# Last attention of a two-block transformer: sink additions, gate splits and two weight splits to GpSimd, first output panel brought forward among the units

## What is computed

```python
def sink_softmax(scores, sink):
    m = sink
    for s in scores:
        m = jnp.maximum(m, jnp.max(s, axis=-1))
    exps = [jnp.exp(s - m[..., None]) for s in scores]
    den = jnp.exp(sink - m)
    for e in exps:
        den = den + jnp.sum(e, axis=-1)
    return tuple(e / den[..., None] for e in exps)
...
    o = o.reshape(bsz, t_lat, AT_Q).astype(h_lat.dtype)
    y_lat = (o * jax.nn.silu(zl)) @ w_out
```

## Time and profile before

| what | us |
|---|---|
| median of 3 runs (1966.79 to 1968.38) | 1968.23 |
| the profiled execution's own time | 1967.3 |
| its span, first to last instruction | 1965.1 |
| units in full flow, 1888.2 to 1930.2 | 42.0 |
| output panels, 1939.1 to 1961.5 | 22.4 |

### The profile page before, as it was taken

The page is one execution under the profiler, slowest core; times in us unless marked ns, Lnnn a source line. Parts: engine busy times, 40 slices in busy tenths (PEclk is TensorE's granted clock), DMA queues, the critical chain, the costliest instruction groups (busy, mean ns, idle before and its releaser), DMA issues. The chain is left out here.

```text
span 1965.1 us, 31270 instructions
## 1 busy us (share of the span) xinstructions
PE 1927.1 (98%) x12652; PEld 1618.6 (82%) x12652; DVE 1303.8 (66%) x2407; ACT 904.7 (46%) x1635; POOL 52.4 (3%) x78
## 2 busy tenths in 40 slices
PE   7999999999999999999999999999999999999998
PEld 5788668889888888898689899998887788888867
DVE  5547777857886665667766777675566464555886
ACT  4446863325423232355764655443443432234685
POOL 0000000001000000000000000000000000001000
PEclk9999999999999999999999999999999999999999
DMA  8322016543545455443139455554311133432411
GB/s 314 117 85 100 18 52 233 179 160 108 193 175 207 177 193 191 166 150 108 54 136 336 172 191 196 177 186 161 119 54 54 65 118 119 150 128 86 150 45 44
DMA packets 53583, 278.39 MB, mean 142 GB/s; under 512 B 4536, under 2 KB 19128, under 8 KB 24512
## 3 DMA queue, kind: packets, MB, share of 16 engines
q1 hardware_dynamic: 47168, 265.50, 37.5%
q10 hardware_dynamic: 6128, 10.03, 1.7%
q0 software_dynamic: 144, 0.85, 0.1%
HBM read 274.26 MB, written 2.11 MB: 141 GB/s over the span
## 5 line engine op out<-in xcount | busy, mean ns | idle before, releaser
L640 PE MATMUL ps<-t 128*128 128x512 f32 (+1 forms) x1936 | 665.2, 344 | 2.4 <-DVE t L2035 2.4
L642 PE MATMUL ps<-t 128*128 128x512 f32 (+1 forms) x1936 | 659.0, 340 | 0.0
L641 PE MATMUL ps<-t 128*128 128x512 f32 (+1 forms) x1936 | 659.0, 340 | 0.0
L2035 DVE TENSOR_TENSOR t<-t 128x1024 fp32r<-128x1024 f32 (+2 forms) x370 | 413.9, 1159 | 153.1 <-ACT t L1386 152.2
L1386 ACT ACTIVATE t<-t 128x1024 fp32r<-128x1024 f32 (+3 forms) x376 | 358.3, 1001 | 194.3 <-PE ps L642 142.6
L640 PEld LDWEIGHTS ps<-t 128*128 128x128 f32 x1936 | 363.6, 188 | 52.5 <-issue 5.1
L642 PEld LDWEIGHTS ps<-t 128*128 128x128 f32 x1936 | 363.6, 188 | 42.5
L641 PEld LDWEIGHTS ps<-t 128*128 128x128 f32 x1936 | 363.7, 188 | 41.8 <-issue 0.7
L2021 DVE TENSOR_TENSOR t<-t 128x256 f32<-128x256 f32 (+9 forms) x622 | 227.9, 386 | 134.3 <-ACT t L1770 31.2
L2030 DVE SCALAR_TENSOR_TENSOR t<-t 128x256 f32<-128x256 f32 (+4 forms) x372 | 272.8, 765 | 34.1 <-ACT t L1491 21.9
L1491 ACT ACTIVATE t<-ps 128x512 f32<-128x512 f32 (+2 forms) x239 | 112.9, 494 | 289.2 <-PE ps L642 187.3
(11 more groups left out here) (191 smaller groups left out, 2278.4 us busy)
## 6 DMA issues: line engine op xcount, KB each, us to landing
t<-in_panels SPq DMA_DIRECT2D x231, 1024.0 KB, 4.9
t<-in_panels SPq DMA_DIRECT2D x12, 768.0 KB, 4.4
t<-in_panels SPq DMA_DIRECT2D x16, 512.0 KB, 3.6
t<-in_window ACTq DMA_DIRECT2D x4, 768.0 KB, 4.5
t<-gates_between ACTq DMA_DIRECT2D x4, 512.0 KB, 4.8
t<-in_panels SPq DMA_DIRECT2D x1, 1088.0 KB, 5.0
t<-in_ctxT SPq DMA_DIRECT2D x1, 1024.0 KB, 6.7
t<-in_xT SPq DMA_DIRECT2D x1, 1024.0 KB, 8.9
```

The lines of the kernel that those rows point to most:

```text
L640: e.matmul(o, hi[:, k, w], xh[:, c0:c1], start=k == 0, stop=False)
L641: e.matmul(o, hi[:, k, w], xl[:, c0:c1], start=False, stop=False)
L642: t = e.matmul(o, lo[:, k, w], xh[:, c0:c1], start=False, stop=k == p.nk - 1)
L2035: e.tensor_tensor(p.half(p.split(wlo), a), p.half(raw[p.slot], a), p.half(p.split(whi), a).bitcast(F32), ALU.subtract).then_inc(*up(ve, (" ...
```

## The change

- `atz` 3 and `atw` 0 go into `POOL_PANELS`: their `lo` is made on POOL. A new POOL function `sink_units` also takes the sink's addition, the denominator's addition, and the whole of `gate_hi` and `gate_lo` (a copy and a subtraction) for the first seven blocks.
- The gate of panel 3 is written as z / (1 + exp(-z)): ACT takes the exponential (no other table), POOL adds 1, DVE takes the reciprocal and multiplies. ACT loads the exponential's table between the query blocks. On DVE the gate moves from i = 1 to i = 2.
- On DVE the second unit's scaling comes ahead of the third unit's maximum.
- The query blocks go into banks 4 to 7; only four of them come ahead of the units, the other four after the scores of unit 0. Gate(3) goes into banks 6 and 7.
- ACT makes the hi of `atw` 0 ahead of the units. PE does the products of `atw` 0 for blocks 0 to 5 within steps 16 to 18, then block 6, two blocks of `atw` 1, block 7, and the rest.

```diff
-POOL_PANELS = [("uq", 0, 0), ("uq", 1, 0), ("atkv", 0)]
+POOL_PANELS = [("uq", 0, 0), ("uq", 1, 0), ("atkv", 0), ("atz", 3), ("atw", 0)]
...
+                query_features(0)
+                def among(i):
+                    if i == 0:
+                        query_features(4)
+                    if i == 1:
+                        gate(3, (6, 7))
+                    if i >= 16:
+                        out_products(0, ((0, 1, 2), (3, 4), (5,))[i - 16])
...
+                softmax("A", at_units(), aPT, among)
+                out_products(0, (6,))
+                out_products(1, (0, 1))
+                out_products(0, (7,))
+                out_products(1, range(2, 8))
...
-                        e.activation(sz[:, c, :], banks(("atz", c))[:, 0:256], ACT.Sigmoid).then_inc(*up(se, ("asig", c)))
+                        f, m = (ACT.Sigmoid, 1.0) if a < 3 else (ACT.Exp, -1.0)
+                        e.activation(sz[:, c, :], banks(("atz", c))[:, 0:256], f, scale=m).then_inc(*up(se, ("asig", c)))
...
                 for c in range(8):
+                    if c == 4:
+                        own()
+                        e.activation(root[:, :], epst[:, :], ACT.Exp).then_inc(*up(se))
...
+                hi_to(at["atw", 0].i)
                 softmax("A", at_units(), aPT, ast, among_units)
...
                 for i in range(n_u + 4):
+                    early = s == "A" and i == 2
+                    if early:
+                        scale(i)
                     if i < n_u:
+                        maximum(i)
+                    if 1 <= i <= n_u and not early:
+                        scale(i)
...
-                        e.wait_ge(*done(("asig", c)))
+                        e.wait_ge(*done(("asig" if a < 3 else "one more", c)))
+                        if a == 3:
+                            e.reciprocal(sz[:, c, :], sz[:, c, :]).then_inc(*up(ve))
+                            own()
                         tt(sz[:, c, :], banks(("atz", c))[:, 0:256], sz[:, c, :], ALU.mult, ("read", ("atz", c)))
...
+            def sink_units():
+                units = at_units()
+                spot = spots(units)
+                lo(at["atw", 0], (0,))
+                for i in range(len(units) + 3):
+                    if i == 2:
+                        for c in (6, 7):
+                            e.wait_ge(*done(("asig", c)))
+                            e.tensor_scalar(sz[:, c, :], sz[:, c, :], 1.0, None, ALU.add).then_inc(*up(po, ("one more", c)))
+                    if 1 <= i <= len(units):
+                        r, es = ast[1][:, spot[i - 1]], ast[2][:, spot[i - 1]]
+                        e.wait_ge(*done(("exp", "A", i - 1)))
+                        e.tensor_tensor(r, r, es, ALU.add).then_inc(*up(po, ("den", "A", i - 1)))
+                    if i == 2:
+                        lo(at["atw", 0], (1,))
+                    if i < len(units):
+                        m, es = ast[0][:, spot[i]], ast[2][:, spot[i]]
+                        e.wait_ge(*done(("max", "A", i)))
+                        e.tensor_tensor(es, m, units[i]["sink"], ALU.add).then_inc(*up(po, ("sink", "A", i)))
+                    if i % 2 == 0 and 4 <= i < 18:
+                        c = i // 2 - 2
+                        e.wait_ge(*done(("az", c)))
+                        e.tensor_copy(aYh[:, c, :], sz[:, c, :]).then_inc(*up(po))
+                        e.wait_ge(po.sem, po.n)
+                        e.tensor_tensor(aYl[:, c, :], sz[:, c, :], aYh[:, c, :].bitcast(F32), ALU.subtract).then_inc(
+                            *up(po, ("aylo", c)))
...
             norm_mod("s1", "cl")
+            lo(at["atz", 3])
+            sink_units()
```

More of the change, by code:

```diff
@@ L1358, in attention_layer @@
                                 t.then_inc(*up(pe, ("full", ("atw", 2 * a + j))))
-                    used(p)
+                    if 7 in ks:
+                        used(p)
+                softmax("A", at_units(), aPT, among)
[3 more added lines that the diff above has]
+                out_products(1, range(2, 8))
+                banks.next(4)
+                for a in range(2, 4):
+                    out_products(a, range(8))
             e.wait_ge(*done("ones"))
@@ L1961, in among_units @@
                         gate(3)
-                    if i in (16, 17):
-                        hi_to(at["atw", i - 16].i)
+                    if i == 17:
+                        hi_to(at["atw", 1].i)
+                hi_to(at["atw", 0].i)
                 softmax("A", at_units(), aPT, ast, among_units)
@@ L2201, in softmax, with maximum @@
                 n_u, spot = len(units), spots(units)
+                def maximum(i):
+                    u, par = units[i], i % 2
+                    both = psum[:, 2 * par:2 * par + 2, :]
+                    e.wait_ge(*done(("full", ("s", s, i))))
+                    m = nm[:, spot[i]]
+                    mv = m.rearrange("p (g x) -> p g x", g=2)
+                    if u["bias"]:
+                        e.wait_ge(*u["bready"])
+                        near = st[2][:, spot[i]]
+                        for g in range(2):
+                            v = banks(("s", s, i, g))[:, 256:512]
+                            e.tensor_tensor_reduce(v, v, u["bias"][g], 1.0, NEG, ALU.add, ALU.max, near[:, g:g + 1]).then_inc(*up(ve))
+                        e.tensor_reduce(mv, both[:, :, 0:256].rearrange("p g (x n) -> p g x n", x=1), AX.X, ALU.max,
+                                        negate=True).then_inc(*up(ve))
+                        own()
+                        stt(m, near, -1.0, m, ALU.mult, ALU.min, ("max", s, i))
+                    else:
+                        e.tensor_reduce(mv, both.rearrange("p g (x n) -> p g x n", x=u["xs"]), AX.X, ALU.max, negate=True).then_inc(
+                            *up(ve, ("max", s, i)))
+                    if u["rms"] is not None:
+                        own()
+                        tt(mv, mv, u["rms"], ALU.mult, ("max", s, i))
+                    if u["sink"] is not None:
+                        own()
+                        tt(m, m, u["nsink"], ALU.min, ("max", s, i))
@@ new lines, in scale @@
+                def scale(i):
+                    u, par = units[i - 1], (i - 1) % 2
+                    r = rs[:, spot[i - 1]]
+                    e.wait_ge(*done(("den" if u["sink"] is not None else "exp", s, i - 1)))
+                    e.reciprocal(r, r).then_inc(*up(ve))
+                    own()
+                    w = 512 // u["xs"]
+                    for g in range(2):
+                        for x in range(u["xs"]):
+                            v = work[:, 2 * par + g, x * w:x * w + w]
+                            c = g * u["xs"] + x
+                            ts(v, v, r[:, c:c + 1], None, ALU.mult, None, ("p", s, i - 1))
@@ L2708, in among_units @@
                 def among_units(i):
-                    if i == 1:
+                    if i == 2:
                         gate(3)
-                    if i in (16, 17):
-                        lo_to(at["atw", i - 16].i)
+                    if i == 17:
+                        lo_to(at["atw", 1].i)
                 softmax("A", at_units(), ast, among_units)
@@ L2764, in gpsimd, with lo @@
         def gpsimd(e):
-            def lo(p):
-                for a in range(2):
+            def lo(p, halves=(0, 1)):
+                for a in halves:
                     e.wait_ge(*done(("hi", p.i, a)))
```

33 lines of the change are left out of this document (17 added, 16 removed).

## The result

| | median us | profiled execution us | its span us |
|---|---|---|---|
| before, beside it on the same chip | 1967.76 | 1967.3 (the one of the earlier trace rows) | 1965.1 |
| with the change | 1973.24 | 1974.73 | 1972.9 |

Slower: the ratio is 1.0028, 95% interval 1.0020 to 1.0037, so +5.5 us (+3.9 to +7.3). 1974.5 was predicted. The profiled execution of the changed kernel lies 1.5 us above its own median, so the terms that follow, all read from it, add up to more than the medians' difference.

The account below looks back on a forecast made before the run. DVE was taken to set the pace of 3.23 us a unit. Start +10.3, pace -1.5 and end -2.3 gave +6.5 us, rounded to about +6.3: median 1974.5 us, 8 in 10 between 1966.5 and 1981.

Parts of the forecast that it names:

- Step 1: Start: POOL's lo of `atz` 3 stalls DVE's second rotation; queries rotated at 1880.4 instead of 1876.4, +4.0 us.
- Step 2: Start: query blocks wait for gate(2)'s reads of their banks; scores of unit 0 at 1882.0 instead of 1878.61, +3.4 us.
- Step 3: Start, ACT: copies, table load and hi of `atw` 0 put the first exponential at 1886.9, not 1881.72, +5.2 us.
- Step 4: Start: late denominator and POOL's half panel delay unit 1's scaling; maximum of unit 2 at 1896.0 instead of 1888.21, +7.8 us.
- the disputed price: Unit 1's scaling on DVE: multiplications by a column wait for POOL's half panel, taken at 2.2 us, bounds 0 and 2.4.
- Step 5: Start: gate(3)'s reciprocals and products, 4.3 us on DVE, put unit 3's maximum at 1901.8; +10.3 us in all by unit 2's transposes.
- The pace: Units 2 to 13: DVE relieved, PE's 3.02 us the floor, 3.09 instead of 3.23 a unit; -1.5 us over eleven.
- The end: Last units: products fill 3.1 us of PE's waits, a new wait of about 0.8 for block 7; -2.3 us.
- hardly meet: Rival at the start: POOL's half panels don't stop DVE; -0.8 us, 1967.4, chance 0.20 with halfway cases up to +3.
- POOL becomes the bound: Rival in the units: small POOL instructions over 0.3 us make its chain the limit; +9 to +14 us, chance 0.15.
- Faster: the start is free: Rival at the start: no conflict, gate's reciprocals fall into a DVE wait; -3.8 to -6 us, 1962 to 1964.4, chance 0.08.

Follow-up runs that it names:

- e1: Changed kernel with the lo of `atz` 3 back on DVE: 1969.93 us, ratio 1.0011 against the kernel before.
- e4: Kernel before the change, with POOL also making the lo of `atz` 3 ahead of DVE, which waits and makes it again: 1973.73 us, ratio 1.0033.
- e2: Changed kernel with POOL's second half of `atw` 0's lo placed after the sink of unit 2: 1972.05 us, ratio 1.0025 against the kernel before.
- e8: e5 with the output panels' products all behind the units: 1963.96 us, ratio 0.9980 against the kernel before.
- e5: Changed kernel with `atz` 3's lo on DVE, `atw` 0's second half lo after unit 2's sink, gate 3 by sigmoid: 1962.01 us, ratio 0.9974 against before.
- e7: Changed kernel with 39 unused matmuls filling PE's long wait ahead of the query transposes: 1972.33 us, ratio 1.0025 against the kernel before.
- e9: e5 with sink and denominator additions and gate splits back on DVE and ACT: 1969.90 us, ratio 1.0012 against the kernel before.
- e10: e9 with DVE making the rest of gated block 6 ahead of the rest of `atw` 1: 1966.46 us, ratio 0.9996 against before.

## Why the prediction held, step by step

The sign, the place and the mechanism were right, and 1973.24 lies 1.3 us from 1974.5; 0.5 of that is the median before, 1967.76 beside it instead of 1968.23, so +5.5 stands against +6.3. But one term was missing, and part of the agreement is luck: errors that cancel. The changed kernel's trace runs ahead of the old one by about 0.6 us before this part (POOL's lo starts at 1872.29, where I had put it at 1872.9).

| step | predicted | in the profile |
|---|---|---|
| 1: queries rotated | 1880.4 | 1879.24 |
| 2: scores of unit 0 | 1882.0 | 1881.53 |
| 3: first exponential | 1886.9 | 1887.86 |
| 4: maximum of unit 2 | 1896.0 | 1897.04 |
| 5: maximum of unit 3 | 1901.8 | 1902.80 |
| transposes of unit 2 | 1904.7 | 1905.54 |
| pace, eleven units | -1.5 | -1.4 |
| end | -2.3 | -2.0 |

- **Step 1** was a little high: the rotations lost 3.5 us, not 4.0. Its own terms give that: 1878.1 and five of 0.36 make 1879.9, +3.5, not 1880.4. I laid only the second rotation beside POOL; the first was already caught, 2.2 of the 3.5. e1 and e4 show the price both ways.
- **Step 2** held: PE's wait of 5.30 ends with gate(2)'s first read, whose banks the query blocks now use.
- **Step 3** was 1.0 short, 1.6 with the earlier trace. Here the missing term enters: at half the clock the scores and the second four blocks take about twice as long, and ACT's copies, hi and exponential stand behind them.
- **Step 4**, the disputed price, was right at its upper end: the pair loses 1.9 us (2.74 against 0.88), and e2 shows that POOL is the cause. The additions of 1 take 0.87, not 0.6, and gate(3)'s matmuls, themselves at full clock, end about 1 us late (1892.6 instead of 1891.5) behind the scores and blocks at half of it; together that puts the denominator at 1893.95 instead of 1892.8.
- **Step 5** held to a tenth: 1902.80 - 1897.04 = 5.76 between the two maxima, against 1901.8 - 1896.0 = 5.8.
- **The pace** came out right for a wrong reason. The floor was not 3.02: the ten units after the third take 2.944 each, and so 2.9 us less than before. The first, at half the clock, takes 1910.28 - 1905.54 = 4.74, 1.5 more than before. The 3.02 that I read between two starts without a printed wait still held about 0.08 of waiting. And POOL's chain, which I had even with DVE's 1.6 us, takes 0.40 + 0.73 + 0.20 = 1.3.
- **The end**, too, is near for a partly wrong reason. The wait for block 7 is 0.32, not 0.8. I had the products fill 3.1 us of waits, but e8 puts only 0.7 of the gain on them: without them its end takes 33.95 us where the kernel before takes 35.16, so 1.2 come with the rest of the change (the wait before the transposes of unit 14 is 1.12 there instead of 1.70).
- **The term left out** is TensorE's clock. I had a wait of PE lengthening by 4 us in step 1 and did not ask what PE does after it; the trace before shows none of it: its waits in this part go to 1.70, and its clock stays at 1.00.

Of the rivals, *hardly meet* falls by the rows of 2.74, 3.51 and 4.72. (Its -0.8 did not follow from its terms either: 4.5 less 1.5 and 2.3 is +0.7.) *POOL becomes the bound* falls by its own condition, small instructions over 0.3 us. POOL by form, 1886 to 1965 (count, busy us, mean ns, idle), beside the earlier trace rows:

```profile
L2841 POOL TENSOR_TENSOR t<-t 128x256 fp32r<-128x256 f32 x7 | 5.1, 729 | 0.6
...
L2829 POOL TENSOR_TENSOR t<-t 128x2 f32<-128x2 f32 x16 | 3.2, 197 | 12.8 <-ACT t L1543 12.8
...
L2839 POOL CAST t<-t 128x256 fp32r<-128x256 f32 x7 | 2.8, 398 | 8.8 <-DVE t L2047 8.8
L2825 POOL TENSOR_SCALAR t<-t 128x256 f32<-128x256 f32 x2 | 1.7, 871 | 1.9 <-ACT t L1966 1.9
```

They take 0.20. *Faster: the start is free* is not what this change does, but it is what e5 is: with the start mended, 1962.01, at the lower end of the 1962 to 1964.4 that this rival gave.

Open is what the low clock costs in the median. Its stretches are no peculiarity of the profile: the mean granted clock is 0.996 in each of the nine executions that the ratio counts, and 0.997 in seven of e7's eight. Within one kernel, executions with less clock are longer: e9's spans are 1965.4 us at a mean of 1.000, 1966.3 to 1966.9 at 0.999 and 1967.6 to 1969.4 at 0.998, e5's 1959.3 to 1960.2, 1961.6 to 1961.7 and 1962.7. That goes with a price for the clock but does not prove one, since a longer wait both lengthens an execution and lowers the clock. The clock's low level and its cause are shown, and so is that the matmuls behind it take longer; its price in the median is not.

## What to carry to other kernels

Small instructions are worth moving from a busy DVE to GpSimd: here the additions of 128x2, at 0.20 us each, and the gate splits of 128x256 gave 3.2 us over eleven units. A long two-input one (2.4 us) did no harm beside a DVE reciprocal or a DVE read of PSUM, and did beside a tensor-tensor and a tensor-scalar; it belongs behind the small ones that others wait for. When an edit lengthens a wait of TensorE, look at the granted clock after the wait and at the durations of the next matmuls, not at the wait alone. Before a difference of 2 us is put down to an edit, see whether it stands where the edit is: most of e8's did not. And price the cheap form of a function on the engine that must finish it: two reciprocals and two additions, with the waits and the lower clock that they brought, cost 5.9 us more here than the table loads that they saved.

## What the runs showed of the hardware that I had not expected

- TensorE's granted clock fell to 0.50 (1.2 GHz) after a single wait of 5.30 us, and again after waits of 1.60 and 2.85 us with 0.71 us of transposes between them (0.52 over 1900.80 to 1910); 1.4 us after the 2.35 us of e9 it fell to 0.50 too. Filling the first wait kept it at 1.00. Shorter waits went either way: at one and the same place it fell after 1.82 us in e1 and 1.79 in e8 (0.73 and 0.69 in 1879 to 1884) and stayed at 1.00 after 1.81 in e5 and 1.80 in e10. What decides there, no run shows.
- On POOL a one-input addition of a constant to 128x256 takes 0.87 us, longer than a two-input subtraction of that size (0.73) and than a rounding copy (0.40).
- Even two-input DVE instructions of 128x2 wait for the end of a POOL instruction. In e5, what is left of the conflict (DVE's row, then POOL's):

```profile
1882.67 2.05 DVE L2047 TENSOR_TENSOR t<-t 128x2 f32<-128x2 f32 x2
...
1882.11 2.40 POOL L2796 TENSOR_TENSOR t<-t 128x1024 fp32r<-128x1024 f32 x1 [52.88 <-ACT t L1409]
```

Two instructions of 0.36 together take 2.05 us and end 0.2 after POOL's. DVE's next work waits for POOL's denominator anyway, so how much of these 1.7 us could be had was not tried.
